# Bias products on eight tensor tiles, one copy of the residual rows and a tenth expert chunk ahead, in a one-core decoder layer step

## What is computed

```
h = x + W_o( sigmoid(g_a) * Mamba2_SSD(n) + sigmoid(g_b) * ShortConv(n) ),  n = RMSNorm(x)
h = h + CrossAttn(RMSNorm(h), mem)        # 4 heads over 256 memory tokens
h = h + MoE(RMSNorm(h))                   # top-4 of 32 experts, clamped SwiGLU
y = RMSNorm(h)

def expert_ffn(xb, w_gu, b_gu, w_dn, b_dn):      # w_gu (1024, 2048), w_dn (1024, 1024), each of 32 experts
    gate, up = jnp.split(xb @ w_gu + b_gu, 2, axis=-1)
    gate = jnp.minimum(gate, 7.0); up = jnp.clip(up, -7.0, 7.0)
    return ((up + 1.0) * gate * jax.nn.sigmoid(1.702 * gate)) @ w_dn + b_dn
```

## Time and profile before

| | |
|---|---|
| median of 3 runs | 1424.09 us (1422.95 to 1424.12) |
| profiled execution, its own time | 1423.08 us |
| its span, first to last instruction | 1421.1 us |
| TensorE busy | 1384.3 us, 97% |
| VectorE, ScalarE busy | 447.7 us, 219.2 us |
| transfers | 494.73 MB, mean 348 GB/s |

### The profile page before, as it was taken

One profiled execution on the slowest core, in us unless ns is written; L12 is line 12 of the kernel. 1 busy time (PEld: TensorE's weight loads), 2 busy tenths in 40 slices (PEclk: granted clock), 3 DMA queues, 4 the chain that ended last, 5 costly groups with the idle time before them and its releaser, 6 DMA issues.

```text
span 1421.1 us, 16026 instructions
## 1 busy us (share of the span) xinstructions
PE 1384.3 (97%) x6385; PEld 681.5 (48%) x6385; DVE 447.7 (32%) x906; ACT 219.2 (15%) x406; POOL 28.1 (2%) x48
## 2 busy tenths in 40 slices
PE   8999999999999999999999999999999999999997
PEld 6788887677756633333333333333233332333322
DVE  5634344862471421211321312213112121121213
ACT  2220022051123400101101001011010110100102
POOL 0000002200000000000000000000000000000000
PEclk9999999999999999999999999999999999999999
DMA  7643435975379599999999999999999999999995
GB/s 253 203 158 129 148 119 176 349 274 223 119 268 406 218 411 387 429 428 428 428 428 428 428 428 428 429 428 428 428 429 428 429 428 428 429 428 428 428 427 231
DMA packets 69782, 494.73 MB, mean 348 GB/s; under 512 B 8443, under 2 KB 9875, under 8 KB 45149
## 3 DMA queue, kind: packets, MB, share of 16 engines
q1 hardware_dynamic: 64652, 477.55, 81.6%
q0 software_dynamic: 4368, 15.53, 3.0%
q10 hardware_dynamic: 724, 1.11, 0.2%
HBM read 486.12 MB, written 8.22 MB: 348 GB/s over the span
## 4 chain that ended last, share of the span: by engine, by line
PE 81%; DMA 15%; DVE 2%; issue 1%; ACT 1%; ACTq 0%; SPq 0%; DVEq 0%
PE bank L1460 77%; DMA flat<-in_w_gate_up 6%; DMA ring<-in_w_gate_up 6%; PE bank L1471 4%; DMA tokT<-in_w_down 2%; DVE wide L1387 1%; DMA ring<-in_w_in 1%; ACTq L608 0%; ACT wide L605 0%; DVE wide L1392 0%; ACT wide L596 0%; PE bank L1917 0%; DVE wide L1443 0%; ACT L615 0%; ACT L645 0%
## 5 line engine op out<-in xcount | busy, mean ns | idle before, releaser
L1460 PE MATMUL bank<-ring,wide 128*64 128x512 f32 (+2 forms) x1696 | 405.3, 595 | 7.3 <-DMA ring<-in_w_gate_up 6.7
L1460 PE MATMUL bank<-wide 128*64 128x512 f32 (+5 forms) x908 | 272.1, 570 | 11.0 <-DVE wide L1387 7.2
L1460 PE MATMUL bank<-tokT,ring 128*128 128x264 f32 x1152 | 266.0, 389 | 2.2 <-DMA ring<-in_w_in 2.2
L1460 PEld LDWEIGHTS bank<-ring,wide 128*64 128x64 f32 (+2 forms) x1696 | 132.5, 140 | 255.8 <-issue 240.1
L1460 PEld LDWEIGHTS bank<-tokT,ring 128*128 128x128 f32 x1152 | 217.3, 191 | 44.1 <-issue 5.4
L1460 PEld LDWEIGHTS bank<-wide 128*64 128x64 f32 (+3 forms) x908 | 92.3, 155 | 170.2 <-issue 116.4
L596 ACT ACTIVATE wide<-bank 64x512 f32<-64x512 f32 (+3 forms) x105 | 58.8, 561 | 334.5 <-PE bank L1460 212.5
L1411 DVE TENSOR_SCALAR wide<-bank 128x512 f32<-128x512 f32 x32 | 22.1, 692 | 271.3 <-PE bank L1460 271.3
L1460 PE MATMUL bank<-flat,wide 128*64 128x512 f32 (+2 forms) x408 | 92.3, 589 | 3.7 <-DMA flat<-in_w_gate_up 3.7
L1460 PE MATMUL bank<-conv,wide 128*64 128x512 f32 (+1 forms) x400 | 91.1, 596 | 0.3 <-ACT wide L596 0.3
L865 ACT ACTIVATE wide<-wide 128x512 f32<-128x512 f32 x32 | 20.2, 630 | 448.0 <-DVE wide L1411 448.0
(11 more groups left out here) (259 smaller groups left out, 749.3 us busy)
## 6 DMA issues: line engine op xcount, KB each, us to landing
ring<-in_w_gate_up SPq DMA_DIRECT2D x64, 2048.0 KB, 27.1
ring<-in_w_down SPq DMA_DIRECT2D x32, 2048.0 KB, 28.4
flat<-in_w_gate_up SPq DMA_DIRECT2D x16, 2048.0 KB, 27.3
conv<-in_w_gate_up SPq DMA_DIRECT2D x16, 2048.0 KB, 26.3
tokT<-in_w_gate_up SPq DMA_DIRECT2D x16, 2048.0 KB, 27.7
wide<-in_w_gate_up SPq DMA_DIRECT2D x16, 2048.0 KB, 26.8
ring<-in_w_in SPq DMA_DIRECT2D x15, 2048.0 KB, 11.8
wide<-in_w_down SPq DMA_DIRECT2D x8, 2048.0 KB, 25.5
```

Source lines behind the costliest of these rows:

```text
L1460: last[0] = pe.matmul(out, lhsT, rhs, start=start, stop=stop)
```

## The change

Four edits go together.

- The gate-and-up bias rows are loaded a second time, with neighbouring row blocks of 32 exchanged (`bgu_crossed`, in the memory of the old convolution states, now `states`), by four loads of 64 KB on SyncE. The second expert's bias products take this copy and the exchanged rows of the one-hot matrix. So the eight products of a pair stand on eight different 32x64 tiles; before, both experts' products stood on the same four.
- The token rows are kept once, unscaled, in `xtok`. The norm factor `rr` is multiplied into every selection matrix instead, by one more VectorE product in each `select`; ScalarE's four scaling copies go, and one more root of one column is taken for rows 32 to 39. The first pair's sums read `xtok` and write `acc`. The region of `acc` and `ytok` is thus free until the first sum.
- That region becomes slot 9 for one chunk: ten chunks are ahead, chunk 5 in slot 9, behind a wait for the stored values (`v_out`), since these lay in that memory. The refills of the ring begin with g = 10.
- The first scatter reads the 32 rows of `b_down` where they were loaded, with the gates' 32 rows. The copies of them into `ytok` and the two memsets on POOL go. The load of the final gain waits for that scatter.

The diff, cut to its core:

```diff
-        msT = sb("msT", [P, XB, 24])
-        ssT = sb("ssT", [P, KB, 16])
+        states = sb("states", [P, CW])
+        bgu_crossed = states
...
+        before_acc = moe[:, 0:4 * D]
         acc = cut(3 * D).rearrange("p (t n) -> p t n", t=3)
+        ytok = cut(D)
+        xtok = [cut(D), cut(D)]
...
-        FIRST_SLOT = [0, 1, 2, 6, 3, 4, 5, 7, 8, 0, 1, 2]
-        AHEAD = 9
+        FIRST_SLOT = [0, 1, 2, 6, 3, 9, 4, 5, 7, 8, 0, 1]
+        AHEAD = 10
...
-            for j, name, k in ((2, "so", 1), (4, "so", 1), (5, "so", 3), (0, "so", 3), (1, "xo", 3), (3, "xo", 7)):
+            filled(sp, "so", 0)
+            for q in range(4):
+                sp.dma_start(bgu_crossed[32 * q:32 * q + 32, :], a["b_gate_up"][0][:, (q ^ 1) * CW:(q ^ 1) * CW + CW])\
+                    .then_inc(S["crossed_in"], 16)
+            for j, name, k in ((2, "so", 1), (4, "so", 1), (5, "so", 3), (0, "so", 3), (9, "so", 3), (1, "xo", 3), (3, "xo", 7)):
                 filled(sp, name, k)
+                if j == 9:
+                    sp.wait_ge(S["v_out"], 16)
                 first_chunk(FIRST_SLOT.index(j))
...
-            for g, done_stages in zip(range(AHEAD, AHEAD + 8), (1, 2, 3, 5, 6, 7, 8, 9)):
+            for g, done_stages in zip(range(AHEAD, AHEAD + 8), (1, 2, 3, 5, 7, 8, 9, 10)):
                 sp.wait_ge(S["stage_done"], done_stages)
                 refill(g, g // 12)
             with sp.Fori(0, n * (PAIRS // 2) + (PAIRS // 2 - 1)) as it:
-                for g in range(17, 41):
+                for g in range(18, 42):
                     sp.wait_ge(S["stage_done"], it * 24 + (g - 7))
...
-            sp.wait_ge(S["ytok_ready"], 2)
+            sp.wait_ge(S["scat_read"], 5)
...
-            pool.memset(ytok, 0.0).then_inc(S["scr_zero"], 1)
-            pool.memset(gT, 0.0).then_inc(S["scr_zero"], 1)
...
+                    s.wait_ge(S["v_out"], 16)
                     raw_tokens(0)
...
-            done(s.activation(rr[0:TS, 2:3], b[0:TS, 2:3], ACT.Sqrt, bias=eps[0:TS, 0:1], scale=1.0 / D), "rs")
+            s.activation(rr[0:TS, 2:3], b[0:TS, 2:3], ACT.Sqrt, bias=eps[0:TS, 0:1], scale=1.0 / D)
+            done(s.activation(rr[32:32 + TS, 2:3], b[0:TS, 2:3], ACT.Sqrt, bias=eps[0:TS, 0:1], scale=1.0 / D), "rs")
             raw_tokens(1)
-            emptied(s, "xtok", 4)
-            s.wait_ge(S["v_out"], 16)
-            s.wait_ge(S["rr_ready"], 1)
-            done(copy(xtok[32:32 + TS, 2, 0:512], filled(s, "xtok", 5)[0:TS, 0:512], rr[0:TS, 2:3]), "xtok", 5)
-            copy(xtok[0:TS, 2, 0:512], acc[0:TS, 2, 0:512], rr[0:TS, 2:3]).then_inc(S["xtok_ready"], 1)
-            for t, n in TILES_P:
-                copy(xtok[0:n, t, :], acc[0:n, t, :], rr[0:n, t:t + 1]).then_inc(S["xtok_ready"], 1)
...
-            s.wait_ge(S["scr_zero"], 2)
-            for h in range(2):
-                copy(ytok[0:E, 512 * h:512 * h + 512], bdn[:, 512 * h:512 * h + 512]).then_inc(S["ytok_ready"], 1)
...
-                ranked(selT, e0).then_inc(S["sel_ready"], 1)
+                st(ranked(selT, e0))
+                v.tensor_tensor(out=selT, in0=selT, in1=bc(rr[:, 0:3], P), op=ALU.mult).then_inc(S["sel_ready"], 1)
...
-            pe.wait_ge(S["xtok_ready"], 3)
...
-                            q = slice(32 * (2 * b + h), 32 * (2 * b + h) + 32)
-                            mm(bank[2 * e + b][64 * h:64 * h + 64, :], onehot[q, 64 * e:64 * e + 64], bgu[q, :], True, False)
+                            rows = 32 * (2 * b + (h ^ e))
+                            mm(bank[2 * e + b][64 * h:64 * h + 64, :], onehot[rows:rows + 32, 64 * e:64 * e + 64],
+                               (bgu, bgu_crossed)[e][rows:rows + 32, :], True, False)
...
-                scatter(at)
+                if bias_rows:
+                    scatter(at, E, bdn)
+                else:
+                    scatter(at)
```

More of the change, by code:

```diff
@@ L280, in build @@
         slot_full = [sem(f"slot_full{i}") for i in range(6)]
-        moe_full = [sem(f"moe_full{i}") for i in range(9)]
+        moe_full = [sem(f"moe_full{i}") for i in range(10)]
         x_in = [sem(f"x_in{t}") for t in range(3)]
@@ L332, in build @@
         mslot += [x.rearrange("p (k n) -> p k n", k=8) for x in (
-            first_acts, tokT[:].rearrange("p s a b -> p (s a b)")[:, 0:4096], wide[:, GB * T:GB * T + 4096])]
+            first_acts, tokT[:].rearrange("p s a b -> p (s a b)")[:, 0:4096], wide[:, GB * T:GB * T + 4096], before_acc)]
         RING = [0, 1, 2, 3, 4, 5, 7, 8]
-        FIRST_SLOT = [0, 1, 2, 6, 3, 4, 5, 7, 8, 0, 1, 2]
-        AHEAD = 9
+        FIRST_SLOT = [0, 1, 2, 6, 3, 9, 4, 5, 7, 8, 0, 1]
+        AHEAD = 10
         def cache(name, i):
@@ L1377, in _, with accumulate @@
             n = v.value_load(npass[0:1, 0:1], min_val=0, max_val=MAXP - 1)
-            v.wait_ge(S["xtok_ready"], 3)
+            emptied(v, "xtok", 5)
             n0, order = st.n, [None, (0, 0), (0, 1), (1, 0), (1, 1)]
-            def accumulate(at, j, last=False):
+            def accumulate(at, j, last=False, fresh=False):
                 v.wait_ge(S["scat_full"], at(5, j + 1))
@@ L1387, in accumulate @@
                         ins = v.tensor_tensor(out=acc[0:TS, 2, 512 * h:512 * h + 512] if last else acc[rows, 2, 0:512],
-                                              in0=bank[6][rows, :], in1=acc[rows, 2, 0:512], op=ALU.add)
+                                              in0=bank[6][rows, :], op=ALU.add,
+                                              in1=xtok[2][rows, 0:512] if fresh else acc[rows, 2, 0:512])
                     return ins.then_inc(S["scat_read"], 1)
@@ L1391, in accumulate, with experts @@
                 dst = acc[:, t, 512 * h:512 * h + 512]
-                return v.tensor_tensor(out=dst, in0=bank[6 + j % 2][:, :], in1=dst, op=ALU.add)\
-                    .then_inc(S["scat_read"], 1)
-            def experts(at, pair, after, final=False):
+                return v.tensor_tensor(out=dst, in0=bank[6 + j % 2][:, :], op=ALU.add,
+                                       in1=xtok[t][:, 512 * h:512 * h + 512] if fresh else dst).then_inc(S["scat_read"], 1)
+            def experts(at, pair, after, final=False, fresh=False):
                 if not final:
@@ L1973, in turn_rows, with scatter @@
                     last[0].then_inc(S["xgt_turned"], 1)
-            def scatter(at):
-                pe.wait_ge(S["ytok_ready"], at(4, 2))
+            def scatter(at, k=P, rows=ytok):
+                if rows is ytok:
+                    pe.wait_ge(S["ytok_ready"], at(4, 0))
                 pe.wait_ge(S["gT_ready"], at(1, 1))
                 for h in range(2):
-                    mm(bank[6][32 * h:32 * h + TS, :], gT[:, TP:T], ytok[:, 512 * h:512 * h + 512])
+                    mm(bank[6][32 * h:32 * h + TS, :], gT[0:k, TP:T], rows[0:k, 512 * h:512 * h + 512])
                 last[0].then_inc(S["scat_full"], 1)
@@ L1985, in scatter @@
                         pe.wait_ge(S["scat_read"], at(5, j - 1))
-                    mm(bank[6 + j % 2][:, :], gT[:, t * P:t * P + P], ytok[:, 512 * h:512 * h + 512])
+                    mm(bank[6 + j % 2][:, :], gT[0:k, t * P:t * P + P], rows[0:k, 512 * h:512 * h + 512])
                     last[0].then_inc(S["scat_full"], 1)
@@ L1996, in _, with experts @@
             pe.wait_ge(S["bias_in"], 128)
+            pe.wait_ge(S["crossed_in"], 64)
             pe.wait_ge(S["passes_ready"], 1)
             n = pe.value_load(npass[0:1, 0:1], min_val=0, max_val=MAXP - 1)
-            def experts(at, pair, it=None, final=False):
+            def experts(at, pair, it=None, final=False, bias_rows=False):
                 def landed(j):
@@ L2073, in experts @@
                 down(1)
-            experts(first_pair, 0)
+            experts(first_pair, 0, bias_rows=True)
             with pe.Fori(0, n * (PAIRS // 2) + (PAIRS // 2 - 1)) as it:
```

52 lines of the change are left out of this document (27 added, 25 removed).

## The result

The changed kernel took 1427.71 us (median of 8 runs, 1425.99 to 1431.54) where the kernel before took 1423.67 (8 runs, 1422.50 to 1426.26): a ratio of 1.0032, 95% interval 1.0021 to 1.0043. It is slower, by about 4 us, and lies above the predicted range. Its profiled execution took 1426.27 us with a span of 1424.3, so it shows 3.2 us of it.

The account below looks back on a forecast made before the run. Weight transfers, unbroken from stage 9, were taken to bound the kernel. Terms +0.2, +0.59 and −0.86 gave −0.1 us, so 1423.0 from the profiled 1423.08, stated as 1424.0 because the runs' median lies 1.0 higher; range 1419.0 to 1426.0.

Parts of the forecast that it names:

- The bound: Whole kernel: transfers set the end, at stage 9 (chunk 16 issued) + 865.6 us of stream + 18.3 us of tail.
- The tenth chunk: Loads ahead of stage 9: one more chunk ahead gains 0, since refill 16 waits for stage 9 in both kernels.
- The hole: Transfer queue ahead of stage 9: hole before 474 about 5 us shorter, new one of some 5 us between 518 and 524.
- The third root: ScalarE, before it releases the bank of the sums: one more root, +0.2 us, bounds 0 and 0.24.
- the selection's product: VectorE, ahead of the first gather: norm factor multiplied into each selection, +0.59 us, bounds 0.5 and 0.7.
- the bias block: Eight gate-and-up bias products on TensorE: two rounds instead of four, −0.86 us, only one block counting before stage 9.
- TensorE's waits for weights: From 541 to the end: doubled from 13.1 to 26 us, the first at about 866 instead of 992.
- The step that failed: First pair's scatter: 32 rows of down bias instead of 128, same 512 columns, 0, ±0.2 us for another tile shape.
- sign of being wrong: Prediction wrong if the queue is busy through 537, the rate differs from 428, or stage 9 moves by over 2 us.
- Rival C: Ahead of the first gather: 0.7 us more TensorE idling lowers the granted clock, 3.2 us lost, 1427.2 us; chance 0.08.

Follow-up runs that it names:

- crossed alone: Kernel before plus only the second copy of the bias rows and the crossed bias tiles; 1423.02 us, ratio 0.9993.
- the short scatter: Kernel before with only its first scatter cut to the 32 rows of the down bias; 1426.69 us, ratio 1.0018.
- 64 rows: Changed kernel with the first scatter on 64 rows, 32 of bias and 32 of zeros; 1426.57 us, ratio 1.0019.
- late-bias kernels: Down bias added in the last pair's scatter, not the first's: kernel before with crossed bias products, 1422.18 us; changed kernel, ten chunks ahead, 1421.69 us.
- nine-ahead kernel that binds at chunk 3: Down bias in the last pair, scattered behind its first chunk, nine chunks ahead, router part of the kernel before; 1419.44 us, ratio 0.9965.
- full-rows kernel: Changed kernel with only the first scatter back on 128 rows, zeros below the 32 bias rows; 1424.23 us, ratio 0.9999.
- 96-row kernel: Changed kernel with the first scatter on 96 rows, 32 of bias and 64 of zeros; 1424.73 us, ratio 1.0003.
- nine-ahead kernel: Changed kernel without its tenth chunk, refills as before the change; 1428.07 us, ratio 1.0031.
- ten-ahead kernel with the early last scatter: Changed kernel, ten chunks ahead, down bias added in the last pair, scattered behind its first chunk; 1419.04 us, ratio 0.9963.

## Why the prediction was wrong

**The bound: right.** In ten of the thirteen profiled executions the span is stage 9 plus 883.9 to 884.7 us (the prediction's 865.6 + 18.3 = 883.9). Some of them: 537.25 and 1421.1 before, 539.59 and 1424.3 after, 536.07 and 1420.5 crossed alone, 540.53 and 1424.5 with the short scatter, 542.68 and 1427.3 with 64 rows. The other three are the two late-bias kernels whose last pair had no slack left (887.0 and 888.4) and the nine-ahead kernel that binds at chunk 3 (886.0), each with its reason in its trace.

**The tenth chunk, 0: right.** Nine instead of ten leaves 1428.07 against 1427.71 us. The hole moved to where it was said to (0 GB/s from 521, stage 7 at 526.45).

**The third root +0.2, the selection's product +0.59, the bias block −0.86: right**, measured as +0.25, +0.60 and −0.83. With the scatter on 128 rows the sum, −0.1 us, gave 1424.23 us where 1424.0 was predicted. TensorE's waits for weights are 23.5 us (10.2 + 6.2 + 6.2 + 0.9) where 26 were expected, the first of them at 847 us where 866 was. The estimate from the Trainium skill, "TensorE: Matmul & The Clock Gate", Part 3 on packing small matmuls, had the block at 1.12 us; the trace has 1.04, so no such loss is seen with eight tiles of 32x64.

**The step that failed** is "The first scatter takes 32 rows of the down bias as they lie instead of 128 rows, with the same 512 columns: 0, ±0.2 for another tile shape." The products themselves are as long as before. The same page of the Trainium skill, section "Why this matters for your kernels", says that a single product of 32 rows takes the time of one with 128; until the clock falls the trace agrees, 2.08 against 2.09 us for six records. What the step missed is the granted clock: it goes to the lower level behind these products, for 3 to 4 us in the changed kernel's trace (1.7 us lost) and for about 7 us in three others (3.4 us lost). By the medians the 32 rows cost 2.8 us in the kernel before and 3.5 us in the changed kernel. Going back to 128 rows removes the slowdown (ratio 1.0032 to 0.9999), and the 32 rows alone make one (1.0018). Stage 9 moved by 2.34 us, over the 2 us that the prediction gave as a sign of being wrong.

**Rival C** named the clock, but looked for idle time ahead of the first gather and held the 4.20 of 6 us busy at a clock of 1.00 against it. TensorE did wait 0.52 us there, with a clock of 1.00 from 484 to 492. The fall came at 520, behind a wait of 0.43 us that the kernel before has as well, in microseconds in which TensorE was busy throughout. The busy share was the wrong row to judge by: it reads the same for products of 32 rows and of 128. Rival C's time, 1427.2 us, is near the result by luck. The prediction asked of every added wait what it does to the clock, and never of a changed tile shape.

What stays open: the median of the changed kernel is 3.5 us above the full-rows kernel, and the changed kernel's trace shows 1.7 us of it: against the 96-row kernel, whose opening is the same (the load into `conv` at 437.84 and 437.89), stage 9 is 1.69 us later (539.59 against 537.90). Whether the unprofiled executions lose more clock behind the scatter, as those with 32 rows in the kernel before and with 64 rows did, or somewhere else, is not shown: the mean granted clock on record for each execution (0.993 by median in the changed kernel, 0.997 with full rows) is that of the whole span, opening and tail included.

## What to carry to other kernels

Do not take rows away from full-width products in a run as long as this one (six products, 5.5 us) because "the zeros are wasted": the products get no shorter, and the clock behind them can fall. Shorter runs of few rows did no harm in the kernel before: four records of 32 rows and 512 columns (1.13 us), eight times between 377 and 416, stand at a clock of 1.00, and so do the 8-row products at the head of the gathers. Read the granted clock in windows of 1 us around every place whose tile shape changes, and not only the busy share. And once the end is a stream of transfers, look for the event that starts it unbroken: work moved from ahead of that event to a place where the engine waits for the stream later is worth up to its whole length (the scatter's 5.5 us ahead of stage 9 gave 5.2 us with ten ahead, from 1424.2 to 1419.0, and 3.6 with nine, from 1423.0 to 1419.4, by medians of different sessions), work saved behind that event is worth nothing (fifteen of the sixteen shorter bias blocks), and the new place must lie ahead of the waits that are to cover it.

## What the runs showed of the hardware

The granted clock of TensorE fell to 0.50 toward the end of the six float32 products with 32 or 64 rows and 512 columns (5.5 us with the wait of 0.4 us between them), in the trace of each of the four kernels that had them, and stayed at 1.00 with 96 and 128 rows in the same place, with zeros in the rows not used. But for that wait, which the kernels that kept 1.00 have too, TensorE was busy in the records throughout. The clock came back to 1.00 during stage 7, under products of 128 rows.

The same level turned up in single executions in places where most have 1.00, ahead of the first pair: between 476 and 484 in the profiled runs of the full-rows kernel, the nine-ahead kernel and two of the late-bias kernels, and between 482 and 494 in those of the 64-row kernel and of the ten-ahead kernel with the early last scatter. The first gather of the latter lasts 7.46 us instead of 4.76:

```profile
484.68 2.16 PE L1936 MATMUL bank<-bgu,ident 128*128 128x256 f32 x6
486.77 7.46 PE L1479 MATMUL bank<-wide 8*128 8x512 f32 x12
```

```profile
488.00:490.00 2.00, 2.00 (x4) 0.71 (x3) 1.72 (x10) 0.00 (x0) 0.00 (x0) 0.50 1.05 445
```

Small products for the ranks, short waits and the gather's products of 8 rows stand there. It seems to go with the execution more than with the kernel: it shows with three roots and with two, and that run took 1422.06 us where the median of its kernel is 1419.04, so a part of the spread of these kernels' times may come from it. One execution of each kernel was traced, which does not show it. What decides it in an execution was not tried.
